# Token rows for a gather written in the order of the feature chunks, from a residual read four columns apart

## The chip, the core and the metric

The kernel runs on one core of one Trainium2 chip. The metric is the device time of one execution in microseconds; the numbers given are the median of several executions and their extremes. The engines are PE (matrix products; its weight loads are listed apart as PEld), DVE (vector), ACT (activations), POOL and SP (here both issue transfers). The profile is of one execution.

## What is computed

Two transformer blocks on 256 tokens of 2048 features, in float32. The change lies in the second block, in front of its mixture of experts (MoE):

```python
def hierarchical_moe(hn, w_router_group, w_router_expert, w_gate, w_up, w_down):
    t = hn.reshape(b * s, d)                       # 256 tokens, hn = rms_norm(h, ffn_norm)
    g_probs = jax.nn.softmax(jnp.dot(t, w_router_group), axis=-1)
    g_w, g_idx = lax.top_k(g_probs, 1)             # one of 4 groups for a token
    ...                                            # top 2 of the 8 experts of that group, weights comb
    for e in range(N_EXPERTS):
        hid = jax.nn.silu(t @ w_gate[e]) * (t @ w_up[e])
        out = out + (hid @ w_down[e]) * comb[:, e:e + 1]
```

## The kernel before

**Products in three parts.** Every float32 product is made of two rounded halves. A helper splits each weight tile (two chunks of 128 rows by 512 columns) into `whi` (ACT, a copy to fp32r) and `wlo` (DVE, the difference), and PE runs three matmuls for each pair (lines 751 to 753). The raw tiles arrive in eight slots, `raw`, by transfers that SP issues.

**What stands around the change.** The residual `xres` holds the tokens on partitions, in two blocks of 128 (index b), with 2048 features along the row. The feed-forward norm of block two has the key "n4". Its feature chunks are "apart": within a group of 512 features, chunk r holds features r, r+4, r+8, ... (`chunk_cols`, lines 642 to 646), because the expert weights are loaded in that order. After the router's products the order of the work is written out by hand, and each engine goes through its own list:

- ACT: `row_high(0)`, `row_high(1)` (line 1966): `x_hi[b]` = `xres[b]` times `rstd[b]`, rounded to fp32r, one activation of 2048 columns for each b. Each bumps the semaphore `moe_act`. Then a small Exp, and 16 evacuations `ghi` of the gathered chunks (line 1974), and from chunk 9 on the first `whi` splits of the MoE between them.
- DVE: the group choice (lines 2790 to 2794), a wait for `row_high(0)`, `row_low(0, 0)` (line 2798: `x_lo` = scaled residual less `x_hi`, 1024 columns), some 15 small instructions that give each token a slot, the one-hot matrices `slot_is` (line 2825), the order of the experts (`first_expert`, line 2831, for which SP waits before it issues the experts' loads), the other three `row_low`, about 20 small instructions of the expert choice, 8 evacuations `glo` (line 2838), 15 small ones for the weights of the tokens, and 8 more `glo` with the first `wlo` splits (line 2081) between them.
- PE: the gather (lines 1302 to 1315). The four groups have unequal numbers of tokens; the largest is computed on all 256 tokens, the others on 384 gathered slots. For each of 16 chunks PE multiplies the chunk of `x_hi` (the weights, 128 by 128) with `slot_is` (384 columns) for both blocks b, then the chunk of `x_lo`. It goes through chunks 0 to 7 with `x_hi`, then 0 to 7 with `x_lo`, then the same for 8 to 15; a chunk k of 8 or more waits until DVE has emptied the bank of chunk k − 8 (`DVE_GATHER + k - 8`). There are 64 matmuls. Behind them in PE's list stands the first MoE tile, which waits for `wlo` of that tile.

The chunks of `x_hi` and `x_lo` stand in the order of `xres`, so the gather loads its weights from columns four apart.

Of the kernel before, what the change touches and what calls it, by code (L numbers as in the profile page):

```python
# [5 lines left out]
F32 = mybir.dt.float32  # L6
F32R = mybir.dt.float32r
I32 = mybir.dt.int32
ACT = mybir.ActivationFunctionType
ALU = mybir.AluOpType  # L10
AX = mybir.AxisListType

P = 128
D = 2048
TB = 2
DC = D // P
COLS = 512
# [30 lines left out]
SLOTS = 3 * P  # L48
# [50 lines left out]
def program(nc, I, out):  # L99
    ctx = ExitStack()  # L100
    with ctx:
        def sb(name, shape, dt=F32):
            return ctx.enter_context(nc.sbuf_tensor(name, shape, dt))
# [3 lines left out]
        def S(name):  # L107
            if name not in sems:
                sems[name] = ctx.enter_context(nc.semaphore(name))
            return sems[name]  # L110
# [10 lines left out]
        xres = sb("xres", [P, TB, D])  # L121
# [12 lines left out]
        def over_big(name, at, shape):  # L134
            return nc.alloc_sbuf_tensor_at(name, shape, F32R, offset=big_at + 4 * at)
# [12 lines left out]
        bank = [ctx.enter_context(nc.psum_tensor(f"bank{i}", [P, COLS], F32)) for i in range(8)]  # L148
# [146 lines left out]
        moe_pe, moe_act, moe_dve = S("moe_pe"), S("moe_act"), S("moe_dve")  # L295
# [26 lines left out]
        def first_part(p):  # L322

            j = p - GATE_STEP
            if j < 24:
                return j // 8, j % 8, 8
            for i, (at, tiles) in enumerate(((24, 3), (27, 1), (28, 4))):
                if at <= j < at + tiles:
                    return 3 + i, j - at, tiles

        STEPS2, OUT2_STEP = 112, 80
        RX, Q, K, V, RG = 3072, 0, 1024, 2048, 4096
# [180 lines left out]
        slot_is = over_big("slot_is", 2304, [P, TB, SLOTS])  # L513
# [3 lines left out]
        wslot = region(big, 1824, 24).rearrange("p (j n) -> p j n", j=3)  # L517
        ghi, glo = over_big("ghi", 3072, [P, DC, 384]), over_big("glo", 9216, [P, DC, 384])
        x_hi, x_lo = (t[:].rearrange("p (b k) a -> p b (k a)", b=TB) for t in (bhi, blo))
        y_hi, y_lo = (t[:, DC - 2:DC, :].rearrange("p k n -> p (k n)") for t in (ahi, alo))  # L520
        dil_mask = [proj1[:, j, 0:3 * 384].rearrange("p (h n) -> p h n", h=3) for j in range(2)]

# [95 lines left out]
        rstd, square_sums = rows[:, 0:2], rows[:, 16:24]  # L618
# [23 lines left out]
        def chunk_cols(key, k):  # L642

            if "apart" in NORMS[key]:
                return slice(k // 4 * COLS + k % 4, (k // 4 + 1) * COLS, 4)
            return slice(k * P, (k + 1) * P)
# [93 lines left out]
        def _(pe):  # L740
            mm = nc.tensor.matmul
# [98 lines left out]
            for k in range(DC):  # L840
                if k >= 4:
                    pe.wait_ge(S("norm_h"), k - 3)
                for b in range(TB):
                    ins = nc.tensor.transpose(bank[4 + k % 4][:, b * P:(b + 1) * P], xn[:, b, k * P:(k + 1) * P], ident[:])
# [181 lines left out]
            for p in range(STEPS):  # L1026
                if p < GATE_STEP:
                    q, k, tiles, base, n = p // 8, p % 8, 8, 0, n_proj1 + p // 8
                    shi, slo, pair = ahi, alo, 2 * (q % 2)
                else:  # L1030
                    part, k, tiles = first_part(p)
# [270 lines left out]
            for k0 in (0, 8):  # L1302
                for src, stop in ((x_hi, False), (x_lo, True)):
                    if stop:
                        pe.wait_ge(moe_dve, DVE_X + k0 // 4)
                    for k in range(k0, k0 + 8):
                        if k0 and not stop:
                            pe.wait_ge(moe_dve, DVE_GATHER + k - 8)
                        for b in range(TB):
                            ins = mm(bank[k % 8][:, 0:SLOTS], src[:, b, chunk_cols("n4", k)], slot_is[:, b],  # L1310
                                     start=(not stop and b == 0), stop=(stop and b == 1))
                        if stop:
                            ins.then_inc(moe_pe, 1)
# [107 lines left out]
        def _(act):  # L1421
            A = nc.scalar.activation
# [95 lines left out]
            def side_turn(no, n):  # L1518
                act.wait_ge(S("side_mm"), no)
                A(side_t[no][0:n, :], bank[6][0:n, 0:256], ACT.Copy).then_inc(S("side_t"), 1)  # L1520
                act.wait_ge(S("side_done"), no)
# [441 lines left out]

            def row_high(b):
                act.wait_ge(S("x_scale"), NORMS["n4"]["scale"])
                A(x_hi[:, b], xres[:, b], ACT.Identity, scale=rstd[:, b:b + 1]).then_inc(moe_act, 1)
            side_turn(3, 36)
            row_high(0)
            row_high(1)
            act.wait_ge(S("rt_sub"), 1)  # L1970
            A(rt[:, 0:8], rt[:, 0:8], ACT.Exp).then_inc(S("rt_exp"), 1)
# [62 lines left out]
            for i in range(4, 4 * 9 + 4):  # L2034
# [10 lines left out]
                if i >= 10 and (i - 10) % 9 == 0 and (i - 10) // 9 < 4:  # L2045
                    g = (i - 10) // 9
# [6 lines left out]
                if i >= 12 and (i - 12) % 9 == 0 and (i - 12) // 9 < 4:  # L2053
                    g = (i - 12) // 9
# [7 lines left out]
        def _(dve):  # L2062
            V = nc.vector
# [730 lines left out]
            V.tensor_tensor(group_one, hit4, wide(at4, 4), ALU.is_equal).then_inc(moe_dve, 1)  # L2794

            def row_low(b, half):
                cols = slice(half * (D // 2), (half + 1) * (D // 2))
                return V.scalar_tensor_tensor(x_lo[:, b, cols], xres[:, b, cols], rstd[:, b:b + 1],
                                              x_hi[:, b, cols].bitcast(F32), ALU.mult, ALU.subtract)
            dve.wait_ge(moe_act, ACT_X)  # L2800
            row_low(0, 0).then_inc(moe_dve, 1)
            for b in range(TB):
                V.tensor_scalar(lg[:, b], route_raw[:, b], rstd[:, b:b + 1], None, ALU.mult)
# [29 lines left out]
            for b, half in ((1, 0), (0, 1), (1, 1)):  # L2833
                row_low(b, half).then_inc(moe_dve, 1)
# [117 lines left out]
            for i in range(4, 4 * 9 + 4):  # L2952
# [11 lines left out]
                if i >= 10 and (i - 10) % 9 == 0 and (i - 10) // 9 < 4:  # L2964
                    g = (i - 10) // 9
                    dve.wait_ge(evac_act, 2 + n_ple + 2 * g + 1)
                    dve.sem_inc(evac_dve, 1)
                if i >= 12 and (i - 12) % 9 == 0 and (i - 12) // 9 < 4:
                    g = (i - 12) // 9
# [4 lines left out]
                    for b in range(TB):  # L2974
                        o = xres[:, b, g * COLS:(g + 1) * COLS]
                        ins = V.tensor_tensor(o, o, prod[:, b], ALU.add)
# [28 lines left out]
```

## Time and profile before

| | us |
|---|---|
| median of 3 executions | 2917.1 (2914.53 to 2917.4) |
| the profiled execution | 2916.19 |
| its span, first to last instruction | 2914.2 |
| PE busy in the span | 2805.2 (96%) |
| DVE busy | 1939.2 (67%) |
| ACT busy | 1480.6 (51%) |
| mean granted clock of PE | 0.985 |

The page of the profile gives busy time by engine, the span in 40 slices, the chain that ended last and the costliest groups of instructions. A duration in the rows is that of one instruction from its start to its last write; the next instruction of the same engine often starts a little before that, so the distance from start to start is what a row of equal instructions costs. Where a row has xN, its second number is the time from the first start to the last end. "Idle" in square brackets is idle time of the engine before it and what ended it. Granted clock 1.00 is 2.4 GHz, 0.50 is 1.2 GHz.

### The profile page before, as it was taken

What the parts mean: (1) busy time and instruction counts of PE and PEld (TensorE: products, weight loads), DVE (VectorE), ACT (ScalarE), POOL (GpSimd) and SP (SyncE); (2) the same over time, 40 slices, a digit from 0 to 9 for tenths busy, and PEclk for the clock granted to TensorE, in tenths of its full rate; (3) what the DMA queues carried; (4) which work ended last, traced back from release to release, by engine and by line L of the source; (5) the groups of instructions that cost most, each with busy time, mean ns of one, the idle gap of its engine ahead of it and who ended that gap; (6) DMA issues with size and microseconds to landing.
All of it is one profiled execution on the core that took longest, in us unless ns stands there. A gap on an engine that the chain in (4) does not pass through costs nothing.

```text
span 2914.2 us, 37396 instructions
## 1 busy us (share of the span) xinstructions
PE 2805.2 (96%) x12693; PEld 2290.4 (79%) x12693; DVE 1939.2 (67%) x2223; ACT 1480.6 (51%) x1825; POOL 16.6 (1%) x27
## 2 busy tenths in 40 slices
PE   3699999999999999999999999999899999999999
PEld 2587877688888788888888888788788887878787
DVE  6867866677777745554554575766554558989884
ACT  3356454444444544344434456544454447777773
POOL 0000000000000000000000000000000000000000
PEclk9799999999999999999999999999999999999999
DMA  9976877678888566556566575555255569999984
GB/s 333 363 220 220 280 232 248 195 240 281 283 288 279 185 193 193 190 185 196 188 194 189 189 194 145 155 158 178 74 207 187 186 217 358 359 360 361 362 288 137
DMA packets 347808, 676.95 MB, mean 232 GB/s; under 512 B 24280, under 2 KB 114832, under 8 KB 347168
## 3 DMA queue, kind: packets, MB, share of 16 engines
q1 hardware_dynamic: 346048, 669.29, 69.1%
q0 software_dynamic: 1632, 5.95, 0.7%
q8 instruction: 82, 1.34, 0.2%
q14 instruction: 46, 0.38, 0.0%
HBM read 673.04 MB, written 2.10 MB: 232 GB/s over the span
## 4 chain that ended last, share of the span: by engine, by line
PE 88%; DVE 6%; ACT 2%; issue 2%; DMA 0%; ACTq 0%; DVEq 0%
PE bank L751 27%; PE bank L753 27%; PE bank L752 27%; DVE big L2166 2%; DVE wlo L2211 1%; PE bank L780 1%; PE bank L831 1%; ACT whi L1442 0%; DVE wlo L2081 0%; PE bank L1137 0%; PE bank L1008 0%; DMA raw<-in_w_in 0%; PE bank L1359 0%; PE bank L789 0%; PE bank L1223 0%
## 5 line engine op out<-in xcount | busy, mean ns | idle before, releaser
L751 PE MATMUL bank<-whi,ahi 128*128 128x512 f32 x2400 | 957.5, 399 | 38.9 <-DVE wlo L2211 25.9
L753 PE MATMUL bank<-whi,alo 128*128 128x512 f32 x2400 | 940.6, 392 | 0.0
L752 PE MATMUL bank<-wlo,ahi 128*128 128x512 f32 x2400 | 939.8, 392 | 0.0
L2069 DVE TENSOR_TENSOR wlo<-raw,whi 128x1024 fp32r<-128x1024 f32 x540 | 652.5, 1223 | 391.6 <-ACT whi L1436 386.5
L1436 ACT ACTIVATE whi<-raw 128x1024 fp32r<-128x1024 f32 x540 | 566.4, 1059 | 453.5 <-PE bank L753 397.0
L751 PEld LDWEIGHTS bank<-whi,ahi 128*128 128x128 f32 x2400 | 454.2, 189 | 139.7 <-issue 36.4
L753 PEld LDWEIGHTS bank<-whi,alo 128*128 128x128 f32 x2400 | 453.6, 189 | 97.2
L752 PEld LDWEIGHTS bank<-wlo,ahi 128*128 128x128 f32 x2400 | 454.9, 190 | 91.6 <-issue 0.7
L2211 DVE TENSOR_TENSOR wlo<-raw,whi 128x1024 fp32r<-128x1024 f32 x280 | 341.0, 1222 | 200.6 <-ACT whi L1429 198.0
L1429 ACT ACTIVATE whi<-raw 128x1024 fp32r<-128x1024 f32 x280 | 295.1, 1059 | 322.5 <-PE bank L753 258.5
L751 PE MATMUL bank<-whi,bhi 128*128 128x512 f32 x944 | 370.7, 393 | 0.0
L753 PE MATMUL bank<-whi,blo 128*128 128x512 f32 x944 | 367.6, 389 | 0.0
L752 PE MATMUL bank<-wlo,bhi 128*128 128x512 f32 x944 | 367.5, 389 | 0.0
L2081 DVE TENSOR_TENSOR wlo<-raw,whi 128x1024 fp32r<-128x1024 f32 x256 | 300.6, 1221 | 64.4 <-ACT whi L1442 62.8
L1442 ACT ACTIVATE whi<-raw 128x1024 fp32r<-128x1024 f32 x256 | 262.9, 1056 | 83.7 <-PE bank L753 75.7
L751 PEld LDWEIGHTS bank<-whi,bhi 128*128 128x128 f32 x944 | 177.3, 188 | 38.4 <-DVE wlo L2069 2.0
L753 PEld LDWEIGHTS bank<-whi,blo 128*128 128x128 f32 x944 | 177.2, 188 | 37.2
L752 PEld LDWEIGHTS bank<-wlo,bhi 128*128 128x128 f32 x944 | 177.3, 188 | 36.3 <-issue 0.5
L751 PE MATMUL bank<-whi,ghi 128*128 128x512 f32 x384 | 153.9, 401 | 3.2 <-DVE wlo L2081 2.8
L753 PE MATMUL bank<-whi,glo 128*128 128x512 f32 x384 | 150.0, 391 | 0.0
L752 PE MATMUL bank<-wlo,ghi 128*128 128x512 f32 x384 | 149.8, 390 | 0.0
L2166 DVE SCALAR_TENSOR_TENSOR big<-raw,silu_c,big 128x1024 f32<-128x1024 f32 x75 | 96.3, 1284 | 8.3 <-DMA raw<-in_w_ada 1.7
(487 smaller groups left out, 1750.9 us busy)
## 6 DMA issues: line engine op xcount, KB each, us to landing
raw<-in_w_in SPq DMA_DIRECT2D x296, 512.0 KB, 4.5
raw<-in_w_ada SPq DMA_DIRECT2D x192, 512.0 KB, 5.2
raw<-in_w_ffn_in SPq DMA_DIRECT2D x352, 256.0 KB, 3.4
raw<-in_w_expert_gate SPq DMA_DIRECT2D x128, 512.0 KB, 4.6
raw<-in_w_expert_up SPq DMA_DIRECT2D x128, 512.0 KB, 5.6
raw<-in_w_expert_down SPq DMA_DIRECT2D x128, 512.0 KB, 6.0
raw<-in_w_ffn_out SPq DMA_DIRECT2D x88, 512.0 KB, 4.1
raw<-in_w_out SPq DMA_DIRECT2D x64, 512.0 KB, 4.9
```

The lines of the kernel that those rows point to most:

```text
L751: mm(o, shi[:, kc, T], whi[:, s, c], start=st, stop=False)
L752: mm(o, shi[:, kc, T], wlo[:, s, c], start=False, stop=False)
L753: ins = mm(o, slo[:, kc, T], whi[:, s, c], start=False, stop=en)
L780: ins = nc.tensor.transpose(pair_bank(key, j)[:, c * 256 + b * P:c * 256 + (b + 1) * P], NORMS[key].get("src", xres)[:, b, chunk_cols(key, ...
L831: ins = mm(bank[at][:, j:j + 1], src[:, j * P:(j + 1) * P], ones[:, 0:1], start=True, stop=True)
L1429: A(whi[:, u % 4], raw[:, t % 8], ACT.Copy).then_inc(hi_ready, 1)
L1436: A(whi[:, t % 4], raw[:, t % 8], ACT.Copy).then_inc(hi_ready, 1)
L1442: A(whi[:, t % 4].rearrange("p k (h n) -> p k h n", h=2), pair_tile(t), ACT.Copy).then_inc(hi_ready, 1)
L2069: V.tensor_tensor(wlo[:, t % 4], raw[:, t % 8], whi[:, t % 4].bitcast(F32), ALU.subtract)\
L2081: V.tensor_tensor(as_tile(wlo[:, t % 4]), pair_tile(t), as_tile(whi[:, t % 4].bitcast(F32)), ALU.subtract).then_inc(lo_ready, 1)
L2166: V.scalar_tensor_tensor(sums, w, col, sums, ALU.mult, ALU.add).then_inc(lo_ready, 1)
L2211: V.tensor_tensor(wlo[:, u % 4], raw[:, t % 8], whi[:, u % 4].bitcast(F32), ALU.subtract)\
```

## The change

`x_hi` and `x_lo` are written in the order of the chunks, so that the gather reads 128 neighbouring columns as weights. For that ACT and DVE read the residual with a stride of four columns (16 bytes) and write contiguously. Each instruction covers one group of 512 columns (4 chunks of 128): ACT issues four for each block where it issued one, and only the fourth bumps the semaphore; DVE issues two for each half where it issued one, and the second bumps. DVE reads `x_hi`, its second input, contiguously. Nothing else is changed.

```diff
--- before.py
+++ after.py
@@ -517,6 +517,9 @@
         wslot = region(big, 1824, 24).rearrange("p (j n) -> p j n", j=3)
         ghi, glo = over_big("ghi", 3072, [P, DC, 384]), over_big("glo", 9216, [P, DC, 384])
         x_hi, x_lo = (t[:].rearrange("p (b k) a -> p b (k a)", b=TB) for t in (bhi, blo))
+        group_cols = [slice(g * COLS, (g + 1) * COLS) for g in range(4)]
+        by_feature = lambda cols: cols.rearrange("q (p r) -> q r p", r=4)
+        in_chunks = lambda cols: cols.rearrange("q (r p) -> q r p", r=4)
         y_hi, y_lo = (t[:, DC - 2:DC, :].rearrange("p k n -> p (k n)") for t in (ahi, alo))
         dil_mask = [proj1[:, j, 0:3 * 384].rearrange("p (h n) -> p h n", h=3) for j in range(2)]
 
@@ -1307,7 +1310,7 @@
                         if k0 and not stop:
                             pe.wait_ge(moe_dve, DVE_GATHER + k - 8)
                         for b in range(TB):
-                            ins = mm(bank[k % 8][:, 0:SLOTS], src[:, b, chunk_cols("n4", k)], slot_is[:, b],
+                            ins = mm(bank[k % 8][:, 0:SLOTS], src[:, b, k * P:(k + 1) * P], slot_is[:, b],
                                      start=(not stop and b == 0), stop=(stop and b == 1))
                         if stop:
                             ins.then_inc(moe_pe, 1)
@@ -1963,7 +1966,9 @@
 
             def row_high(b):
                 act.wait_ge(S("x_scale"), NORMS["n4"]["scale"])
-                A(x_hi[:, b], xres[:, b], ACT.Identity, scale=rstd[:, b:b + 1]).then_inc(moe_act, 1)
+                for cols in group_cols:
+                    ins = A(in_chunks(x_hi[:, b, cols]), by_feature(xres[:, b, cols]), ACT.Identity, scale=rstd[:, b:b + 1])
+                ins.then_inc(moe_act, 1)
             side_turn(3, 36)
             row_high(0)
             row_high(1)
@@ -2794,9 +2799,10 @@
             V.tensor_tensor(group_one, hit4, wide(at4, 4), ALU.is_equal).then_inc(moe_dve, 1)
 
             def row_low(b, half):
-                cols = slice(half * (D // 2), (half + 1) * (D // 2))
-                return V.scalar_tensor_tensor(x_lo[:, b, cols], xres[:, b, cols], rstd[:, b:b + 1],
-                                              x_hi[:, b, cols].bitcast(F32), ALU.mult, ALU.subtract)
+                for cols in group_cols[2 * half:2 * half + 2]:
+                    ins = V.scalar_tensor_tensor(in_chunks(x_lo[:, b, cols]), by_feature(xres[:, b, cols]), rstd[:, b:b + 1],
+                                                 in_chunks(x_hi[:, b, cols].bitcast(F32)), ALU.mult, ALU.subtract)
+                return ins
             dve.wait_ge(moe_act, ACT_X)
             row_low(0, 0).then_inc(moe_dve, 1)
             for b in range(TB):
```

## Rows read from the trace of the kernel before

**Rows 1.** The page of the profile: busy shares by engine, and the ending chain
```profile
PE 2805.2 (96%) x12693; PEld 2290.4 (79%) x12693; DVE 1939.2 (67%) x2223; ACT 1480.6 (51%) x1825; POOL 16.6 (1%) x27
...
PE 88%; DVE 6%; ACT 2%; issue 2%; DMA 0%; ACTq 0%; DVEq 0%
```

**Rows 2.** Windows after the MoE starts: PE, PEld, DVE, ACT, POOL busy, PEclk, DMA share
```profile
2117.80:2392.00 274.20, 273.20 (x1228) 226.16 (x1229) 141.88 (x141) 125.63 (x138) 0.70 (x1) 1.00 0.55 193
...
2392.00:2565.00 173.00, 171.46 (x754) 137.88 (x753) 154.16 (x153) 129.70 (x146) 0.00 (x0) 1.00 0.97 357
```

**Rows 3.** Timeline around the gather: start us, us, engine, line, operation, tiles, count, idle
```profile
2093.47 3.90 ACT L1966 ACTIVATE bhi<-xres,gl_a 128x2048 fp32r<-128x2048 f32 x2 [0.40 <-PE bank L811]
...
2095.50 1.28 DVE L2798 SCALAR_TENSOR_TENSOR blo<-xres,gl_a,bhi 128x1024 fp32r<-128x1024 f32 x1 [0.97 <-ACT bhi L1966]
...
2100.54 5.51 PE L1310 MATMUL bank<-slot_is,bhi 128*128 128x384 f32 x16 [5.28 <-DVE slot_is L2825]
...
2101.12 3.67 DVE L2798 SCALAR_TENSOR_TENSOR blo<-xres,gl_a,bhi 128x1024 fp32r<-128x1024 f32 x3
...
2104.01 0.36 SPq L478 DMA_DIRECT2D raw<-in_w_expert_gate  x1
...
2108.50 4.29 DVE L2838 SCALAR_TENSOR_TENSOR glo<-bank,gain_ffn,ghi 128x384 fp32r<-128x384 f32 x8
...
2115.09 1.05 ACT L1442 ACTIVATE whi<-raw 128x1024 fp32r<-128x1024 f32 x1
...
2115.40 1.14 DVE L2838 SCALAR_TENSOR_TENSOR glo<-bank,gain_ffn,ghi 128x384 fp32r<-128x384 f32 x2
...
2116.45 1.21 DVE L2081 TENSOR_TENSOR wlo<-raw,whi 128x1024 fp32r<-128x1024 f32 x1
...
2117.81 0.47 PE L751 MATMUL bank<-whi,ahi 128*128 128x512 f32 x1 [0.44 <-DVE wlo L2081]
```

**Rows 4.** Waits of DVE from 2095.5 to 2117.9, and its busy time there
```profile
DVE blo L2798 <- ACT bhi L1966: 1.0, 1, 1.0
...
2095.50:2117.67 22.17, 20.62 (x71) 0.77 0.49 189
```

**Rows 5.** Weight loads in the timeline, strided then contiguous, and two matmul starts
```profile
2109.56 3.83 PEld L1310 LDWEIGHTS bank<-slot_is,bhi 128*128 128x128 f32 x16
...
273.93 1.76 PEld L831 LDWEIGHTS bank<-ones,acc 128*128 128x128 f32 x15
...
2128.11 0.39 PE L751 MATMUL bank<-whi,ahi 128*128 128x512 f32 x1
...
2128.34 0.39 PE L752 MATMUL bank<-wlo,ahi 128*128 128x512 f32 x1
```

**Rows 6.** The timeline of ACT: four activations of 256 columns with a per-partition scale
```profile
1794.30 1.70 ACT L1902 ACTIVATE big<-rnn_r,stat 128x256 f32<-128x256 f32 x4
```

**Rows 7.** Single lines: duration ns min/median/max of reduces, strided one first
```profile
L2849 DVE TENSOR_REDUCE big<-big x1: 269/269/269, 2105.4 to 2105.4; 128x16 f32<-128x64 f32 x1
...
L2858 DVE TENSOR_REDUCE big<-big x2: 169/169/169, 2106.4 to 2107.8; 128x2 f32<-128x16 f32 x2
...
L2662 DVE TENSOR_REDUCE stat<-big x8: 286/286/288, 1860.2 to 1974.6; 128x1 f32<-128x128 f32 x8
```

**Rows 8.** The transposes' weight loads: columns contiguous (first) and four apart (second)
```profile
L780 PEld LDWEIGHTS bank<-ident,xres x16: 138/140/143, 1713.2 to 1723.1; 128*128 128x128 f32 x16
...
L780 PEld LDWEIGHTS bank<-ident,xres x32: 196/211/220, 2040.8 to 2087.3; 128*128 128x128 f32 x32
```

**Rows 9.** Windows over the granted clock, and the PE idle time before it fell
```profile
2100.50:2106.70 6.20, 6.16 (x19) 6.16 (x20) 5.82 (x17) 0.21 (x1) 0.00 (x0) 0.50 0.27 87
...
1823.40:1826.80 3.40, 1.48 (x6) 1.23 (x7) 1.95 (x4) 3.37 (x4) 0.00 (x0) 1.00 0.17 17
...
1826.80:1830.20 3.40, 3.36 (x9) 2.16 (x8) 2.66 (x4) 3.40 (x5) 0.00 (x0) 0.50 0.41 139
...
1825.32 0.50 PE L751 MATMUL bank<-whi,ahi 128*128 128x512 f32 x1 [2.01 <-DVE wlo L2069]
```


## Prediction

> **What bounds the kernel now.** The page comes first: PE is busy for 96% of the span, and 88% of the chain that ended last is PE [rows 1]. So a microsecond counts if it moves the products of PE, and I ask when PE starts on the MoE, the first large stage behind the change. Behind that start nothing takes up a delay: PE is busy for 273.2 of 274.2 us in the stage with all tokens, and the next stages run at 357 GB/s with the transfer engines 97% busy; their loads are issued as PE frees the eight slots, so they move along with PE [rows 2]. A delay of the start is a delay of the end.
>
> Next, the timeline around the gather [rows 3]. The first MoE matmul starts at 2117.81 after 0.44 us of idle that ended with DVE's `wlo`; this ran from 2116.45. The reader should then follow DVE's rows backwards: `glo` from 2115.40, eight `glo` from 2108.50, three `row_low` from 2101.12, the first `row_low` at 2095.50, which waited 0.97 us for ACT's `row_high(0)`. The view of waits says that from there to 2117.9 DVE waited for nobody but that once, and the window has 20.62 us of work in 22.17 [rows 4]. The missing 1.55 us are some 45 gaps of 34 ns between small instructions that each need the one before. So the start of the MoE is ACT's `row_high(0)`, then 22.2 us of DVE work end to end. PE's gather, the long row of matmuls beside it, isn't in this chain: it waits for DVE at its start (5.28 us) and is done before DVE is.
>
> **Part 1: the gather's weight loads (removed: their stride).** With columns four apart 16 loads take 3.83 us; less one duration of 0.33 and over 15 steps that is 0.233 us from start to start. Fifteen loads of 128 neighbouring columns take 1.76 us: (1.76 − 0.19)/14 = 0.112 [rows 5]. A load of 0.112 us is hidden under its matmul, which then sets the step. 512 columns take 0.23 us at the full clock [rows 5], 0.213 of it for the columns at 2.4 GHz, so 384 columns take 0.160 + 0.014 = 0.174. At the low clock the columns alone need 0.32 us, more than either load: (5.51 − 0.52)/15 = 0.33 [rows 3]. The first 19 of the 64 matmuls run at a granted 0.50 [rows 9] and gain nothing; the other 45 gain 0.059 each, 2.7 us of PE. None of it reaches the end, because DVE covers it: PE finds the banks of chunks 8 to 15 occupied until `glo` frees them, 0.53 us a chunk against 2 × 0.174 = 0.35, and after the gather it waits for `wlo`.
>
> **Part 2: ACT in four pieces (added).** The DVE chain hangs on the end of `row_high(0)`, so its growth counts in full. A 2048-column instruction takes 3.90 − 1.99 = 1.91 us from start to start [rows 3]. Four of 256 columns with a per-partition scale take (1.70 − 0.50)/3 = 0.40 [rows 6]. That is 0.84 ns a column and 0.18 us fixed; 512 columns take 0.62, four 2.46. Growth without a stride penalty: 0.55 us. `row_high(1)` grows by as much; PE needs it only with `slot_is` and DVE for the second `row_low`, and both come later than its end (below), so it costs nothing.
>
> **Part 3: DVE in two pieces.** 1024 columns take (3.67 − 1.28)/2 = 1.195 us, 384 columns (4.29 − 0.61)/7 = 0.526 [rows 3]. So 1.045 ns a column and 0.125 us fixed; a half in two pieces costs 0.125 more. All four `row_low` are in the chain: 0.50 us.
>
> **Part 4: reading four columns apart (added; no wide row of DVE or ACT shows it).** Three rows bound it. The nearest by engine is DVE's reduce at line 2849, whose inner axis steps 8 columns: 64 elements in 269 ns [rows 7]. Reduces without that step take 169 for 16 and 286 for 128, so 64 should take 219 to 220; the excess is 49 ns. It is 0.77 ns an element, or, as 48 of its reads are steps inside a row of four, 1.02 ns a step: one more period of the 1.04 ns that DVE spends on a column. The second is PE on this very data and stride: (0.233 − 0.112)/128 = 0.95 ns more for each column. The third speaks against: the transposes' loads of `xres` take 211 ns instead of 140 [rows 8], 0.55 ns more a column, and they still deliver one in under a nanosecond, faster than DVE takes one; if only the supply limits, DVE wouldn't notice. So the bounds are 0 (a gain is excluded: the same columns are read, and no strided row is faster than its contiguous one) and about 1.0 ns a column. I take the upper part, since the only row of the engine itself shows it. DVE: 4 × 1024 × 1.02 = 4.2 us. ACT, which has no strided row: PE's 0.95 × 2048 = 1.95 us. Writes stay contiguous and cost nothing new.
>
> The Trainium skill ("SBUF — State Buffer", the note on cachelines in the section "Door 1: The DMA port swizzle") says that SBUF has lines of 16 bytes, and that a read that goes to a new line each time pays a penalty; it gives no size. A stride of four float32 columns is a new line for each element. By that rule both engines pay, and the sum is the forecast's; were the rule true of PE alone, the sum would be the second rival's. The trace agrees on PE and on DVE's one reduce.
>
> **The sum.** 0.55 + 0.50 + 4.2 + 1.95 = 7.2 us later start of the MoE. Its sides: `row_high(1)` would end at 2093.5 + 2 × 4.4 + 0.1 = 2102.4, before PE's start, which moves by 2.5 + 1.2 = 3.7 us to 2104.2, and before the second `row_low`. PE does 16 + 16 matmuls by about 2113 and then idles until `glo(0)` is written at 2108.50 + 7.2 + 0.6 = 2116.3. The clock may fall in those 3 us. Even then 19 matmuls at the low clock (as many as at the gather's start) and 13 at the high one end at 2116.3 + 6.2 + 2.3 = 2124.8, just ahead of DVE's `wlo` at 2124.9. At most, with all 32 slow, they end at 2126.5, 1.6 later. SP's loads of the experts wait for `first_expert`, are issued from 2104.01 [rows 3] and would be 3.7 us later; the first `whi` read them at 2115.09 and will now at 2122, 11 us of room as before plus 3.5. No wait, semaphore or transfer is added. The profiled execution takes 2916.2, 0.9 under the median; 2916.2 + 7.2 = 2923.4, and for the median 2917.1 + 7.2 = 2924.3 us (+0.25%).
>
> **Rivals.**
> - *Only DVE pays for the stride.* 0.55 + 0.50 + 4.2 = 5.2: 2922.3. For it: DVE has a row, ACT none. Against: both read the same memory. Taking 0.77 ns on both engines instead gives 1.05 + 4.7 = 5.8, about 2922.9, and belongs to the forecast.
> - *Neither pays.* Only the pieces cost: 1.05 us, 2918.2, no difference that can be measured. For it: the transposes. It decides if the memory gives a strided float in less than DVE's 1.04 ns.
> - *The same, and PE's clock falls.* The faster gather ends near 2117.0, and PE then idles until 2118.9. The trace has such a case: idle for 2.01 us until 1825.32, and from 1826.8 a granted 0.50 for 3.4 us [rows 9]. A step of 512 columns costs 0.43 us there instead of 0.23, so 3.4 us lose 3.4 × (1 − 0.23/0.43) = 1.6: 2919.8.
> - *The other side: the gather sets the start.* If DVE's row of work had slack that the view of waits doesn't show, and PE's last gather matmul released the MoE, 2.7 us would be won, less 0.7 for the later `slot_is`: 2915.1. It decides if DVE's rows are stretched by waits on PE and ACT; against it stand the one wait in 22 us [rows 4] and PE's own idle time of 0.44 us in front of the MoE [rows 3].
> - *The change doesn't do what it says*: the weight loads keep their 0.233 us, because something but the stride makes them slow. The time is the same as in the other cases, since PE's gain isn't in the sum.
>
> **How the numbers follow.** Both engines pay 0.50 (2924.3, its own range 2922.6 to 2926.3); DVE alone 0.15 (2922.3); neither 0.24 (2918.2); neither, and the clock falls 0.06 (2919.8); the gather sets the start 0.05 (2915.1). The likeliest is 2924.3. The three times shown spread over 2.9 us, so a median can be off by a good microsecond, and a measurement can tell about 0.2%, 5.8 us, from no change. The low end reaches over most of the "neither" case, 2917.0; the high end is the forecast with most of a fallen clock, 2926.3. Slower by over 0.2% means above 2922.9: 0.85 of the first case and 0.3 of the second, 0.46 with a little for worse luck. Faster by 0.2% needs more than the gather has to give: 0.02. The rest, 0.52, is within 0.2%: the forecast lies just above the bound, and the other cases below it.
>
> **What would show it.** In the changed profile: the ACT row of line 1966 (eight pieces) with a step of 0.62 us if free and 1.1 if strided reads are slow; DVE's row of line 2798 (eight pieces) with 0.66 or 1.18; PE's steps in the second half of the gather at 0.174 where it isn't waiting, and idle time in front of chunk 8 that ends with `glo`; DVE still without a wait up to the first `wlo`; the first MoE matmul near 2125 (2119 if nobody pays). I am wrong if DVE waits for PE or ACT in that stretch, if the first MoE matmul moves and the end doesn't, or if the strided rows cost less than 0.5 or more than 1.2 ns a column extra.

## The result, and the profile after

The changed kernel takes 2921.89 us (median of 20 executions, 2920.11 to 2923.57); the kernel before, run beside it, 2915.7 (20 executions, 2914.44 to 2917.4). The ratio is 1.002 with a 95% interval of 1.0014 to 1.0026: 6.2 us slower, and the interval reaches from 4.1 to 7.6. The profiled execution has a span of 2920.4 us, 6.2 more than before.

The page of the profile shows next to nothing of it. PE has as many matmuls, DVE four instructions more, ACT six, and their shares stay [rows 1]:

```profile
PE 2804.5 (96%) x12693; PEld 2288.5 (78%) x12693; DVE 1943.2 (67%) x2227; ACT 1485.7 (51%) x1831; POOL 16.6 (1%) x27
```

The timeline of the changed kernel around the gather (start us, us, engine, line, operation, tiles, count, idle before it) is where to look; it answers [rows 3]:

```profile
2093.06 8.85 ACT L1970 ACTIVATE bhi<-xres,gl_a 128x512 fp32r<-128x512 f32 x8 [0.40 <-PE bank L814]
2097.56 2.16 DVE L2803 SCALAR_TENSOR_TENSOR blo<-xres,gl_a,bhi 128x512 fp32r<-128x512 f32 x2 [3.44 <-ACT bhi L1970]
...
2103.47 4.35 PE L1313 MATMUL bank<-slot_is,bhi 128*128 128x384 f32 x16 [8.62 <-DVE slot_is L2831]
2104.05 6.38 DVE L2803 SCALAR_TENSOR_TENSOR blo<-xres,gl_a,bhi 128x512 fp32r<-128x512 f32 x6
...
2107.66 2.94 PE L1313 MATMUL bank<-slot_is,blo 128*128 128x384 f32 x16
...
2114.13 4.29 DVE L2844 SCALAR_TENSOR_TENSOR glo<-bank,gain_ffn,ghi 128x384 fp32r<-128x384 f32 x8
...
2114.80 5.41 PE L1313 MATMUL bank<-slot_is,bhi 128*128 128x384 f32 x16 [4.20 <-DVE glo L2844]
...
2120.05 2.94 PE L1313 MATMUL bank<-slot_is,blo 128*128 128x384 f32 x16
2120.60 1.05 ACT L1979 ACTIVATE ghi<-bank,gain_ffn 128x384 fp32r<-128x384 f32 x2 [5.80 <-PE bank L1313]
2121.22 1.15 DVE L2844 SCALAR_TENSOR_TENSOR glo<-bank,gain_ffn,ghi 128x384 fp32r<-128x384 f32 x2
...
2122.63 1.22 DVE L2086 TENSOR_TENSOR wlo<-raw,whi 128x1024 fp32r<-128x1024 f32 x1 [0.27 <-ACT whi L1445]
...
2124.00 0.47 PE L754 MATMUL bank<-whi,ahi 128*128 128x512 f32 x1 [1.01 <-DVE wlo L2086]
```

One number serves for all comparisons below: the *distance* from the start of `row_high(0)` to the first matmul of the MoE. It was 2117.81 − 2093.47 = 24.34 us and is 2124.00 − 2093.06 = 30.94, 6.6 more. What follows is untouched: from that matmul to the end of the span it is 796.4 us in both. What precedes isn't touched by the change either, but it moves: in the twelve profiled executions of this document `row_high(0)` starts between 2091.71 and 2094.59 us (the two here differ by 0.4). That is why the distance is a sharper measure than the time.

Reading down the rows: the ACT row starts before DVE's, and DVE waits 3.44 us for it instead of 0.97. The DVE row of eight pieces has become long (2.16 and 6.38 us for what took 1.28 and 3.67). PE does the gather's first half, the 16 matmuls with `x_lo` in 2.94 us at 0.174 us each, and then sits idle for 4.20 us. Its next 16 take 5.41. The clock explains this (windows of the changed kernel: PE, PEld, DVE, ACT and POOL busy, granted clock, transfers; it answers [rows 9]):

```profile
2106.40:2110.60 4.20, 4.20 (x24) 3.88 (x23) 4.17 (x6) 0.00 (x0) 0.00 (x0) 1.00 0.64 216
...
2113.20:2119.90 6.70, 5.10 (x16) 5.08 (x17) 6.29 (x21) 1.60 (x5) 0.00 (x0) 0.50 0.91 366
2120.00:2123.00 3.00, 2.99 (x17) 2.67 (x16) 2.46 (x9) 2.40 (x5) 0.00 (x0) 1.00 0.00 0
```

It was 1.00 until 2112.0, fell to 0.50 (1.2 GHz) while PE sat idle, at about 2113.2, and was back at 2.4 GHz at 2120. And now DVE does wait once more inside its stretch, which it never did before [rows 4] (waits of DVE in the changed kernel from 2097.6 to 2124.1: us in total, times, longest):

```profile
DVE blo L2803 <- ACT bhi L1970: 3.4, 1, 3.4
DVE wlo L2086 <- ACT whi L1445: 0.3, 1, 0.3
```

The chain of work that ended last, between 2114 and 2124, goes through PE's slow gather accordingly, and not through DVE:

```profile
2114.21 0.54 DVE glo L2844
2114.80 5.78 PE bank L1313 x18
2120.60 0.39 ACT ghi L1979
...
2121.65 0.96 ACT whi L1445
2122.63 1.24 DVE wlo L2086
```

The 6.6 us, added up along the two timelines: 2.46 in ACT's `row_high(0)`, 0.86 in the first half of `row_low`, 2.70 in the other three, 0.56 in this new passage through the gather, and hundredths for the rest. The 0.56 is read from the start of the eight `glo` to the first matmul of the MoE: 2124.00 − 2114.13 = 9.87 us, where it was 2117.81 − 2108.50 = 9.31. Of it 0.2 lies in front of `glo` of chunk 8, which now has to wait for `ghi` of that chunk, by a gap too short for the view of waits, and 0.36 between it and `wlo`. The durations of the pieces, from the lines of the changed kernel (ns, min/median/max):

```profile
L1970 ACT ACTIVATE bhi<-xres,gl_a x8: 1182/1192/1201, 2093.1 to 2100.7; 128x512 fp32r<-128x512 f32 x8
...
L2803 DVE SCALAR_TENSOR_TENSOR blo<-xres,gl_a,bhi x8: 1111/1123/1150, 2097.6 to 2109.3; 128x512 fp32r<-128x512 f32 x8
```

From start to start they take (8.85 − 1.19)/7 = 1.09 us on ACT and (6.38 − 1.12)/5 = 1.05 on DVE.

### The profile page after: what moved, and what is told of

The parts are those of the page before. It is cut to its first block, busy times and chain, and to the rows that moved or that the text cites. A ratio compares the mean times of both kernels' runs of the same rounds, so it can differ in the third digit from the quotient of the medians.

```text
span 2920.4 us, 37406 instructions
## 1 busy us (share of the span) xinstructions
PE 2804.5 (96%) x12693; PEld 2288.5 (78%) x12693; DVE 1943.2 (67%) x2227; ACT 1485.7 (51%) x1831; POOL 16.6 (1%) x27
## 4 chain that ended last, share of the span: by engine, by line
PE 88%; DVE 6%; ACT 2%; issue 1%; DMA 1%; ACTq 0%; DVEq 0%
PE bank L754 28%; PE bank L756 27%; PE bank L755 27%; DVE big L2171 2%; DVE wlo L2216 1%; PE bank L783 1%; DMA raw<-in_w_in 1%; PE bank L834 0%; ACT whi L1445 0%; DVE wlo L2086 0%; PE bank L1140 0%; ACT whi L1432 0%; PE bank L1011 0%; PE bank L1362 0%; PE bank L792 0%
```

## Experiments

Each expectation was written before its kernel ran. Ratios are to the kernel before, with 95% intervals.

### The gather alone

```diff
-mm(bank[k % 8][:, 0:SLOTS], src[:, b, chunk_cols("n4", k)], slot_is[:, b],
+mm(bank[k % 8][:, 0:SLOTS], src[:, b, k * P:(k + 1) * P], slot_is[:, b],
```

> Of the change only the gather's read of x_hi and x_lo from 128 neighbouring columns; ACT and DVE write them as before, so the gathered features stand in another order than the experts' weights expect (the permutation is left out). Measure: the distance from the start of row_high(0) to the first MoE matmul, 24.34 us before and 30.94 after. Theory (DVE's row of work sets the start, PE's gain is covered): 24.3 us, weight loads no longer the limit, 0.174 us a matmul at the full clock where PE isn't waiting, time within 0.1% of before. Rival (the gather sets the start): 21.6 us, 2.7 us faster. A fallen clock of PE in the longer idle time before the MoE would show as up to 1.6 us slower.

Measured: ratio 0.9997 (0.9988 to 1.0007), distance 24.34 us, unchanged to the hundredth. The timeline of this kernel shows the gain arising and being waited away:

```profile
2107.91 4.29 PE L1310 MATMUL bank<-slot_is,bhi 128*128 128x384 f32 x16
...
2108.44 0.30 PEld L1310 LDWEIGHTS bank<-slot_is,bhi 128*128 128x128 f32 x2 [0.23 <-DVE glo L2838]
...
2112.05 2.95 PE L1310 MATMUL bank<-slot_is,blo 128*128 128x384 f32 x16
...
2116.56 0.47 PE L751 MATMUL bank<-whi,ahi 128*128 128x512 f32 x1 [1.57 <-DVE wlo L2081]
```

In the kernel before, the matmuls with `x_lo` of the second half were this row:

```profile
2113.48 3.90 PE L1310 MATMUL bank<-slot_is,blo 128*128 128x384 f32 x16
```

They now take 2.95 us for 16 instead of 3.90, but the ones with `x_hi` are let through two by two by `glo` (seven rows like the second), and the MoE is awaited for 1.57 us instead of 0.44 [rows 3]. The rival "the gather sets the start" falls. The clock didn't fall in these 1.57 us or after them: it is 1.00 up to 2122.

### ACT's part alone

```diff
-A(x_hi[:, b], xres[:, b], ACT.Identity, scale=rstd[:, b:b + 1]).then_inc(moe_act, 1)
+for cols in group_cols:
+    ins = A(in_chunks(x_hi[:, b, cols]), by_feature(xres[:, b, cols]), ACT.Identity, scale=rstd[:, b:b + 1])
+ins.then_inc(moe_act, 1)
```

> Of the change only ACT's part: row_high reads with the stride of four columns in four pieces; DVE and the gather stay, so x_lo doesn't match x_hi (the order of features in the gathered rows is not kept). Theory (ACT's time counts in full in front of DVE's row of work): row_high(0) takes 4.47 us instead of 2.00, the distance from its start to the first MoE matmul 24.34 + 2.5 = 26.8 us, time +2.5 us; row_high(1) costs nothing. Rival (most of the 6.2 us is contention between the engines' strided reads): a smaller growth here and in the DVE part alone, the two not adding up to 6.

One remark in it is off: DVE forms `x_lo` as the residual less whatever stands in `x_hi`, so their sum is right in every column and nothing is left out. Measured: distance 26.82 us, +2.47 where 2.5 was expected; ratio 1.0006 (0.9996 to 1.0016), which holds both no change and the expected 1.0009. The DVE rows of this kernel, one of 1.28 and three in 3.67, are those of before; only the wait in front of the first has grown:

```profile
2098.17 1.28 DVE L2803 SCALAR_TENSOR_TENSOR blo<-xres,gl_a,bhi 128x1024 fp32r<-128x1024 f32 x1 [3.45 <-ACT bhi L1970]
```

### DVE's part alone

```diff
-cols = slice(half * (D // 2), (half + 1) * (D // 2))
-return V.scalar_tensor_tensor(x_lo[:, b, cols], xres[:, b, cols], rstd[:, b:b + 1],
-                              x_hi[:, b, cols].bitcast(F32), ALU.mult, ALU.subtract)
+for cols in group_cols[2 * half:2 * half + 2]:
+    ins = V.scalar_tensor_tensor(in_chunks(x_lo[:, b, cols]), by_feature(xres[:, b, cols]), rstd[:, b:b + 1],
+                                 in_chunks(x_hi[:, b, cols].bitcast(F32)), ALU.mult, ALU.subtract)
+return ins
```

> Of the change only DVE's part: row_low reads the residual with the stride of four columns in pieces of 512; ACT and the gather stay, so x_lo is not the remainder of x_hi (features in another order). Theory: four halves of 2.08 us instead of 1.197 each, distance 24.34 + 3.6 = 27.9 us, time +3.6 us. PE's second half of the gather starts 3.6 us later after an idle time; if its clock falls, 0.3 to 1.5 us more. Rival (contention with ACT's strided reads makes DVE slow): pieces near 0.66 us, +0.5.

Measured: distance 28.30 us, +3.96 (3.6 was expected, and 0.3 to 1.5 more if the clock fell); ratio 1.0011 (1.0001 to 1.0021). Its pieces are as long as in the changed kernel, though ACT reads contiguously here and is done before the last six of them start, so it isn't contention between the two:

```profile
2096.11 2.20 DVE L2801 SCALAR_TENSOR_TENSOR blo<-xres,gl_a,bhi 128x512 fp32r<-128x512 f32 x2 [0.97 <-ACT bhi L1969]
...
2102.64 6.46 DVE L2801 SCALAR_TENSOR_TENSOR blo<-xres,gl_a,bhi 128x512 fp32r<-128x512 f32 x6
...
2113.48 4.98 PE L1313 MATMUL bank<-slot_is,bhi 128*128 128x384 f32 x16 [2.31 <-DVE glo L2842]
...
2121.00 1.23 DVE L2084 TENSOR_TENSOR wlo<-raw,whi 128x1024 fp32r<-128x1024 f32 x1 [0.15 <-ACT whi L1445]
```

The last two rows show that the clock's part was in this kernel too: 2.31 us idle, 16 matmuls in 4.98 us, and DVE waits for `whi`. The granted clock is 0.62 in the first 2.5 us of these matmuls (columns as above):

```profile
2113.50:2116.00 2.50, 2.50 (x8) 2.50 (x9) 2.50 (x6) 0.00 (x0) 0.00 (x0) 0.62 1.02 419
```

From the first `glo` to the MoE it takes 2122.37 − 2112.82 = 9.55 us, 0.24 more than the 9.31 of the kernel before. Together the two parts alone give 2.47 + 3.96 = 6.4 of the 6.6 us.

### The pieces alone

```diff
-by_feature = lambda cols: cols.rearrange("q (p r) -> q r p", r=4)
+by_feature = lambda cols: cols.rearrange("q (r p) -> q r p", r=4)
```

(from the changed kernel, with the gather's line as before)

> The change's pieces of 512 on ACT and DVE, but reading contiguously and writing in the order of before, with the gather as before; nothing is left out of the computation. Theory: ACT 0.62 us a piece, DVE 0.66, distance 24.34 + 0.55 + 0.50 = 25.4 us, time +1.0 us. Rival (the pieces, not the stride, carry the cost): ACT 1.09 and DVE 1.04 a piece, distance 30 us.

Measured: distance 25.41 us, +1.06 where 1.05 was expected; ratio 1.0002 (0.9992 to 1.0012). The pieces read contiguously take 0.61 and 0.66 us from start to start, and the durations are 705 and 744 ns against 1192 and 1123 with the stride:

```profile
L1970 ACT ACTIVATE bhi<-xres,gl_a x8: 704/705/721, 2093.0 to 2097.3; 128x512 fp32r<-128x512 f32 x8
...
L2803 DVE SCALAR_TENSOR_TENSOR blo<-xres,gl_a,bhi x8: 742/744/752, 2095.6 to 2104.7; 128x512 fp32r<-128x512 f32 x8
```

So of the 6.6 us, 1.06 are the pieces and the rest is the stride and what it sets off. PE's gather has its strided loads in this kernel, and DVE's pieces are fast beside them, so these don't slow DVE.

### The stride without the pieces

```diff
-for cols in group_cols:
-    ins = A(in_chunks(x_hi[:, b, cols]), by_feature(xres[:, b, cols]), ACT.Identity, scale=rstd[:, b:b + 1])
-ins.then_inc(moe_act, 1)
+A(in_chunks(x_hi[:, b]), by_feature(xres[:, b]), ACT.Identity, scale=rstd[:, b:b + 1]).then_inc(moe_act, 1)
...
+at = slice(half * 256, (half + 1) * 256)
+return V.scalar_tensor_tensor(in_chunks(x_lo[:, b])[:, :, at], by_feature(xres[:, b, cols]), rstd[:, b:b + 1],
+                              in_chunks(x_hi[:, b].bitcast(F32))[:, :, at], ALU.mult, ALU.subtract)
```

> The changed kernel with the stride of four kept and the pieces taken away: one activation of 2048 columns for each block, one DVE instruction for each half, chunk 4g + r of the features at columns 512 r + 128 g; the gather still reads 128 neighbouring columns, nothing is left out. Theory (1.78 ns for each strided column on either engine, plus the fixed part of an instruction): 3.8 us for a row on ACT instead of 4.36 from start to start, 1.95 for a half on DVE instead of 2.08; distance from row_high(0) to the MoE 30.9 - 0.5 - 0.5 = 29.9 us. Rival (the three-dimensional pattern itself or its row starts cost): no gain, or another step per column.

Measured: ratio 1.0019 (1.001 to 1.0029), distance 30.27 us: 0.67 won of the expected 1.0. The instructions did what was expected (from start to start 3.83 us for a row on ACT, 1.97 for a half on DVE). What is missing sits in DVE's waits of this kernel:

```profile
DVE glo L2842 <- ACT ghi L1977: 0.5, 1, 0.5
DVE wlo L2084 <- ACT whi L1445: 0.3, 1, 0.3
```

From the first `glo` to the MoE it takes 10.24 us here, 9.87 in the changed kernel and 9.31 before: 0.37 of what DVE and ACT saved was lost again. PE's second half ran at the low clock (16 matmuls in 5.49 us), and DVE waited behind it.

### Strides of two and of eight columns

```diff
-by_feature = lambda cols: cols.rearrange("q (p r) -> q r p", r=4)
-in_chunks = lambda cols: cols.rearrange("q (r p) -> q r p", r=4)
+by_feature = lambda cols: cols.rearrange("q (p r) -> q r p", r=2)
+in_chunks = lambda cols: cols.rearrange("q (r p) -> q r p", r=2)
```

(and the same with r=8)

> The changed kernel with a stride of two columns (8 bytes) instead of four on both engines, everything else as changed; the features then stand in an order that the experts' weights don't expect (the right permutation is left out). Theory (what costs is that each read goes to a new 16-byte line; at a stride of two, two reads fall into each line): free, ACT 0.62 us and DVE 0.66 a piece as with contiguous reads, distance from row_high(0) to the MoE 25.4 us. Rival (any stride costs): ACT 1.09, DVE 1.04, 30.9 us. In between if a line costs a fixed 1.8 ns and two reads share it: then 0.9 ns a column, hidden behind DVE's 1.04 and just over ACT's 0.84, which would be ACT 0.64.

> The changed kernel with a stride of eight columns (32 bytes), otherwise as e6: the right permutation is left out. Theory (a new line costs 1.8 ns however far it is): ACT 1.09, DVE 1.04 a piece, distance 30.9 us as in the changed kernel. Rival (the cost grows with the distance, by banks or pages): longer pieces.

The lines of the kernel with a stride of two, then of the one with eight:

```profile
L1970 ACT ACTIVATE bhi<-xres,gl_a x8: 730/737/748, 2092.2 to 2096.7; 128x512 fp32r<-128x512 f32 x8
...
L2803 DVE SCALAR_TENSOR_TENSOR blo<-xres,gl_a,bhi x8: 742/744/750, 2094.9 to 2104.0; 128x512 fp32r<-128x512 f32 x8
```

```profile
L1970 ACT ACTIVATE bhi<-xres,gl_a x8: 1195/1198/1213, 2091.8 to 2099.5; 128x512 fp32r<-128x512 f32 x8
...
L2803 DVE SCALAR_TENSOR_TENSOR blo<-xres,gl_a,bhi x8: 1129/1139/1195, 2096.3 to 2108.2; 128x512 fp32r<-128x512 f32 x8
```

A stride of two costs DVE nothing (744 ns, as contiguous) and ACT 0.03 us a piece (0.64 from start to start against 0.61); distance 25.52 us, ratio 1.0003 (0.9992 to 1.0013). A stride of eight costs nearly what four costs: 1.11 us a piece from start to start on ACT and 1.07 on DVE, against 1.09 and 1.05; ratio 1.0022 (1.0012 to 1.0033). Its distance is 30.86 us, no longer than that of the changed kernel although its pieces are, because 0.31 us less is lost in the passage through the gather (9.56 us from the first `glo` to the MoE instead of 9.87). Not the stride as such costs, then, but going to another group of four columns (16 bytes) with each read, and whether that is the next group or the one after hardly matters. The sizes fit one price, about 1.8 ns for each 16-byte group that is opened: at four (1.09 − 0.18)/512 = 1.78 ns a column on ACT and (1.05 − 0.125)/512 = 1.81 on DVE, at eight 1.81 and 1.85; at two, where two columns share it, 0.9, just above ACT's own 0.84 and below DVE's 1.04. And PE's strided weight loads in the gather take 0.233/128 = 1.82 ns a column [rows 5], but its transposes' loads don't fit (last section). Where the columns lie relative to 16-byte boundaries wasn't varied, so that the group is aligned to them is argued, not shown. The Trainium skill's rule ("SBUF — State Buffer", section "Door 1: The DMA port swizzle": lines of 16 bytes, at least two hits in each for full bandwidth) is borne out by DVE at all three strides; ACT pays 0.03 us a piece even with two hits.

### PE kept busy

```diff
+                        if stop and k == 7:
+                            for n in range(30):
+                                mm(bank[7][:, SLOTS:SLOTS + P], x_hi[:, 0, 0:P], slot_is[:, 0, 0:P], start=False, stop=False)
```

> The changed kernel with 30 spare matmuls of 128 columns ahead of the last chunk of the gather's first half (some 3.3 us of PE's 4.2 idle us), into columns of a bank that nobody reads; nothing is left out. Theory (the clock that fell in that idle time made the second half of the gather 2.5 us longer, and this is the 0.5 us that DVE waited for ghi(8) and whi): the granted clock stays 1.00, the second half steps at 0.174 us, DVE's wait in front of the first wlo is gone, distance 30.94 - 0.55 = 30.4 us. Rival (DVE waits there for something else): clock up, distance unchanged. If the spare work delays ACT's ghi(7), it shows in front of glo(7).

Measured: distance 30.42 us, −0.52; ratio 1.0018 (1.0009 to 1.0028). The rows of this kernel (two windows with the columns as above, then the timeline):

```profile
2107.50:2114.60 7.10, 7.10 (x53) 7.10 (x53) 6.62 (x20) 2.78 (x7) 0.00 (x0) 1.00 0.71 261
2115.00:2123.00 8.00, 7.11 (x33) 5.16 (x32) 7.52 (x26) 3.33 (x8) 0.00 (x0) 1.00 0.69 278
```

```profile
2115.88 4.29 PE L1316 MATMUL bank<-slot_is,bhi 128*128 128x384 f32 x16 [0.85 <-DVE glo L2847]
...
2122.12 1.14 DVE L2847 SCALAR_TENSOR_TENSOR glo<-bank,gain_ffn,ghi 128x384 fp32r<-128x384 f32 x2
2123.17 1.22 DVE L2089 TENSOR_TENSOR wlo<-raw,whi 128x1024 fp32r<-128x1024 f32 x1
```

With the clock at 2.4 GHz throughout, DVE's waits are gone, and from the first `glo` to the MoE it takes 2124.53 − 2115.22 = 9.31 us, as in the kernel before. The 0.56 us in the passage through the gather were the fallen clock.

### From the kernel before: slots first, and one half on POOL

```diff
-            dve.wait_ge(moe_act, ACT_X)
-            row_low(0, 0).then_inc(moe_dve, 1)
...
-            for b, half in ((1, 0), (0, 1), (1, 1)):
+            for b, half in ((0, 0), (1, 0), (0, 1), (1, 1)):
```

> From the kernel before, without the change: the first row_low is moved behind the slot instructions of DVE, so that these no longer wait for ACT's row_high(0). Nothing is left out. Theory (the start of the MoE is DVE's work end to end behind what it waits for): the slot instructions start 1.7 us earlier (they then wait only for PE's counts), the moved half adds 1.2 to what follows, distance from row_high(0) to the MoE 24.35 - 0.5 = 23.8 us, time -0.5 us, too little to be measured in the time. PE's gather starts 1.7 us earlier and gains nothing from it. Rival (ACT's row, not DVE's work, sets the start): no change.

Measured: distance 23.82 us, −0.52, as worked out; ratio 0.9998 (0.9989 to 1.0007), too small for the time to show. It agrees with the reading that the wait of 0.97 us in DVE's list [rows 4] is time in front of the MoE.

```diff
+                scaled = region(big, 14208, D // 2)
+                nc.gpsimd.tensor_scalar(scaled, xres[:, 1, cols], gl_a16[:, 1:2], None, ALU.mult)
+                nc.gpsimd.tensor_tensor(x_lo[:, 1, cols], scaled, x_hi[:, 1, cols].bitcast(F32), ALU.subtract)
```

> As e9_slots_first, and one of the four halves of row_low (block 1, second half) is computed by POOL, which is idle, in two instructions; PE's second half of the low part waits for it. Nothing is left out. Theory (DVE's work sets the start, the gather has just about 1.2 us of slack): DVE is relieved of 1.2 us, distance 23.8 - 1.2 = 22.6 us, time -1.7 us; PE's gather then ends about when wlo is ready. Rival (POOL and DVE disturb each other at the memory): DVE's pieces grow while POOL works, and the distance stays over 23.4.

Measured: distance 26.09 us, 1.75 more than before and 2.3 more than with the slots alone; ratio 1.0006 (0.9997 to 1.0015). The theory lost, but not quite as the rival put it. DVE's wide instructions came later and had their usual 1.27 us; three small ones were caught (timeline of that kernel):

```profile
2095.71 3.00 POOL L576 TENSOR_SCALAR big<-xres,gl_a 128x1024 f32<-128x1024 f32 x1 [79.78 <-ACT bhi L1976]
...
2095.85 0.98 DVE L2829 TENSOR_TENSOR big<-big 128x8 f32<-128x8 f32 x1
...
2097.07 0.75 DVE L2833 TENSOR_SCALAR slot_is<-big 128x384 fp32r<-128x384 f32 x2
2097.73 1.00 DVE L2836 TENSOR_SCALAR big<-big 128x4 f32<-128x4 f32 x1
...
2098.79 2.37 POOL L578 TENSOR_TENSOR blo<-big,bhi 128x1024 fp32r<-128x1024 f32 x1
...
2099.15 2.04 DVE L2839 CAST first_expert<-big 128x4 int32<-128x4 f32 x1
```

The same three take 0.17, 0.22 and 0.17 us in the kernel before, so 3.5 us were lost to save 1.2. The last two end within 0.03 us of the end of a POOL instruction. The two `slot_is` beside them take 0.75 us, as in the kernel before.

## Why the prediction was right, point by point

- *Where it counts.* DVE's list, end to end behind ACT's `row_high(0)`, sets the start of the MoE, and a delay there is a delay of the end: shown by the unchanged 796.4 us behind it and by the gather alone, which gained nothing.
- *The gather's loads (part 1).* Forecast 0.174 us a matmul at the full clock; measured 2.94 us for 16, less 0.33 and over 15 steps, 0.174. That it is worth nothing: shown.
- *The pieces (parts 2 and 3).* Forecast 0.55 + 0.50 = 1.05 us; measured alone 1.06.
- *The stride (part 4).* ACT: forecast 1.95 us, priced by PE's strided loads; the pieces' 0.55 off the measured 2.46 leaves 1.91. That this came out so well is luck in part: what carries over from PE is the whole 1.8 ns a column, and not what it is more than PE's contiguous 0.112/128 = 0.875. The two ways agree only because ACT's own 0.84 is so close to that. DVE: forecast 4.2 us, measured 0.86 + 2.70 − 0.50 = 3.06. This term was mis-sized by 1.1 us, at the step that chose between two readings of the one strided reduce: I took 1.02 ns for each step inside a row, where 0.77 an element was right (measured 0.75). The gather's strided loads would have told: with their 1.8 ns for such a column, DVE's excess is 1.8 − 1.04 = 0.76, and not a whole period of its own. The third row of part 4 was read a little too fast: the transposes' strided loads deliver a column in 1.05 ns (last section), which is not under a nanosecond and not faster than DVE's 1.04. The rival that nobody pays had a little less behind it than was said, but the row still doesn't fit the 1.8 ns.
- *PE's idle time and its clock.* The prediction saw both, put the gather's end "just ahead" of DVE's `wlo`, and left it out of the sum. It cost 0.56 us. By the prediction's own sign ("wrong if DVE waits for PE or ACT in that stretch") this point went against it: DVE waited for `whi`. The step that failed looked only at the last matmul: the first `wlo` needs `whi`, which stands on ACT behind `ghi(8)` and `ghi(9)`, and these need the first low matmuls of the second half, not the last.
- *The sum.* 7.2 forecast, 6.6 measured in the distance and 6.2 in the medians: the DVE term too large by 1.1, the clock's 0.56 missing, so two errors of opposite sign hide half of the larger one. The forecast of 2924.3 stood on the median of 2917.1 shown; over 20 executions that is 2915.7. These 1.4 us and the 1.0 between 7.2 and 6.2 make up the 2.4 by which the forecast lies above 2921.9. The prediction gave 0.46 to a kernel slower by over 0.2% and 0.52 to one within 0.2%; the measured ratio of 1.002, with an interval on both sides of that bound, doesn't decide between them.
- *The rivals.* "Only DVE pays" and "neither pays" are refuted by the two lines of the changed kernel, and with "neither pays" goes the rival in which nobody pays and the clock falls in front of the MoE (in the gather alone PE was idle there for 1.57 us, and the clock stayed up). "The gather sets the start" is refuted by the gather alone, and "doesn't do what it says" by the 0.174 us.

## What to carry to other kernels

An instruction that gets faster is worth what the chain through it is worth: follow the releaser of the next large stage backwards, and if an engine works there without a gap, only that engine's work counts. Moving a stride of 16 bytes from PE's weight loads, where it was covered, to reads on ACT and DVE, where it wasn't, made each column take 1.8 ns there instead of the engine's own 0.84 or 1.04. And when an engine is made to wait longer, ask what its clock does in the meantime and who needs its first result afterwards, not only its last.

## What the runs showed of the hardware beyond expectation

- One price in three places: a float32 column read from a new group of 16 bytes takes about 1.8 ns on ACT (1.78), on DVE (1.81) and in the gather's weight loads on PE (1.82). At a stride of two columns DVE reads at its usual rate. It is no price of all reads: the transposes' weight loads read the residual four columns apart too, and eight of them take 1.15 us in the kernel before, (1.15 − 0.21)/7 = 0.134 us from start to start, 1.05 ns a column. No run here says what sets them apart.

```profile
2078.28 1.15 PEld L780 LDWEIGHTS bank<-ident,xres 128*128 128x128 f32 x8
```

- PE's clock fell in or soon after idle times of 2.01 us [rows 9], 2.31 (DVE's part alone) and 4.20 us (the changed kernel), and didn't after 1.57 (the gather alone). The length of the idle time alone doesn't decide: the one of 2.01 us stands in all twelve profiles, and in those of ACT's part alone and of the pieces alone the clock stayed at 1.00 behind it. This is ACT's part alone, where that idle time ends at 1825.53:

```profile
1826.50:1830.00 3.50, 2.25 (x10) 1.54 (x10) 2.71 (x3) 3.50 (x6) 0.00 (x0) 1.00 0.56 152
```

- While POOL ran an elementwise instruction of 1024 columns, three small DVE instructions (one with two tensor inputs, a scalar operation and a cast with one each) took 0.98 to 2.04 us instead of 0.17 to 0.22, and others beside them took their usual time. The Trainium skill ("SBUF — State Buffer", section "🔬 SBUF: two separate sides") says that POOL and DVE share a pair of ports which one instruction holds until it ends, and that DVE needs it with two SBUF inputs or in a two-port mode. The scalar operation and the cast end with POOL's instruction, as they would by that rule, but no row shows in which mode they ran. The one with two inputs, to which the rule applies in any mode, ended 1.9 us before POOL's instruction did. That part isn't explained by the rule, nor by a run here.
